# One level of Strassen's scheme for the output product of a hybrid attention layer

## The reference, cut to what matters

```python
merged = jax.nn.sigmoid(mg_a + b_gate[0]) * y_a + jax.nn.sigmoid(mg_b + b_gate[1]) * y_b
sub = jnp.einsum('bsd,de->bse', merged, w_out)              # 512 x 2048 by 2048 x 2048
out = layer_norm(DN_ALPHA * x.astype(jnp.float32) + sub.astype(jnp.float32), ln_g, ln_b)
```

## Time and profile before

| | |
|---|---|
| median of 3 runs | 1430.04 us |
| the profiled execution, its own time | 1427.57 us |
| its span, first to last instruction | 1425.8 us |
| mean granted TensorE clock | 0.997 |
| PE busy, share of the span | 98% |
| POOL, ACT, DVE busy | 49%, 35%, 26% |
| DMA moved, mean rate | 141.02 MB, 99 GB/s |

### The profile page before, as it was taken

One profiled execution on the slowest core, in us unless ns is written; L12 is line 12 of the kernel. 1 busy time (PEld: TensorE's weight loads), 2 busy tenths in 40 slices (PEclk: granted clock), 3 DMA queues, 4 the chain that ended last, 5 costly groups with the idle time before them and its releaser, 6 DMA issues.

```text
span 1425.8 us, 20252 instructions
## 1 busy us (share of the span) xinstructions
PE 1400.8 (98%) x6692; PEld 1185.1 (83%) x6692; DVE 368.2 (26%) x733; ACT 505.7 (35%) x694; POOL 701.7 (49%) x534
## 2 busy tenths in 40 slices
PE   9999999999999999999999999999999999999996
PEld 7878888778988988898898888888888888888885
DVE  5866565642030112203101101010010100400116
ACT  5455455443342343334234322222222222412122
POOL 4533333355445645544453455355553545554446
PEclk9999999999999999999999999999999999999998
DMA  8422221242333323233342334243342433393222
GB/s 258 122 60 74 79 78 45 73 143 70 89 90 85 89 77 97 66 87 88 85 116 66 88 94 112 74 118 88 88 118 74 118 84 88 113 269 107 91 74 118
DMA packets 191674, 141.02 MB, mean 99 GB/s; under 512 B 17296, under 2 KB 179344, under 8 KB 190736
## 3 DMA queue, kind: packets, MB, share of 16 engines
q1 hardware_dynamic: 191632, 140.47, 34.2%
HBM read 136.21 MB, written 4.19 MB: 98 GB/s over the span
## 4 chain that ended last, share of the span: by engine, by line
PE 92%; DVE 3%; issue 2%; ACT 1%; POOL 0%; DMA 0%; POOLq 0%; DVEq 0%; SPq 0%; ACTq 0%
PE acc L1010 84%; PE ps_out L1090 2%; PE ps_out L1081 1%; PE ps_scores L1034 1%; PE ps_scores L1027 1%; PE ps_turn L1064 1%; PE ps_scores L1010 1%; PE ps_out L1010 1%; DVE q_split L865 1%; PE ps_turn L1069 0%; DMA raw<-xT 0%; ACT q_split L491 0%; POOL z L443 0%; PE ps_scores L1036 0%; PE ps_scores L1035 0%
## 5 line engine op out<-in xcount | busy, mean ns | idle before, releaser
L430 POOL TENSOR_TENSOR w_lo<-raw,w_hi 128x512 fp32r<-128x512 f32 x260 | 342.7, 1318 | 712.5 <-ACT w_hi L457 698.8
L1010 PE MATMUL acc<-x_hi,w_hi 128*128 128x512 f32 x1216 | 479.3, 394 | 2.6 <-DVE q_a L723 2.6
L1010 PE MATMUL acc<-x_hi,w_lo 128*128 128x512 f32 x1216 | 474.3, 390 | 0.0
L1010 PE MATMUL acc<-x_lo,w_hi 128*128 128x512 f32 x1216 | 473.9, 390 | 0.0
L457 ACT ACTIVATE w_hi<-raw 128x1024 fp32r<-128x1024 f32 x256 | 267.8, 1056 | 447.9 <-PE acc L1010 421.3
L431 POOL TENSOR_TENSOR w_lo<-raw,w_hi 128x512 fp32r<-128x512 f32 x260 | 353.0, 1358 | 0.0
L1010 PEld LDWEIGHTS acc<-x_hi,w_lo 128*128 128x128 f32 x1216 | 228.3, 188 | 48.4
L1010 PEld LDWEIGHTS acc<-x_hi,w_hi 128*128 128x128 f32 x1216 | 228.6, 188 | 46.6 <-DVE q_a L723 3.2
L1010 PEld LDWEIGHTS acc<-x_lo,w_hi 128*128 128x128 f32 x1216 | 228.6, 188 | 43.5
L1010 PE MATMUL acc<-w_hi,x_hi 128*128 128x384 f32 (+1 forms) x512 | 185.3, 362 | 0.0
L1010 PE MATMUL acc<-w_hi,x_lo 128*128 128x384 f32 (+1 forms) x512 | 185.2, 362 | 0.0
(11 more groups left out here) (160 smaller groups left out, 1066.1 us busy)
## 6 DMA issues: line engine op xcount, KB each, us to landing
raw<-w_in SPq DMA_DIRECT2D x384, 128.0 KB, 2.3
raw<-w_in SPq DMA_DIRECT2D x256, 96.0 KB, 2.5
raw<-w_out SPq DMA_DIRECT2D x128, 128.0 KB, 2.9
raw<-w_in SPq DMA_DIRECT2D x64, 192.0 KB, 2.7
raw<-w_pa SPq DMA_DIRECT2D x64, 128.0 KB, 2.3
raw<-xT SPq DMA_DIRECT2D x8, 512.0 KB, 4.7
raw<-w_in SPq DMA_DIRECT2D x64, 64.0 KB, 2.2
raw<-w_pb SPq DMA_DIRECT2D x64, 64.0 KB, 2.5
```

Source lines behind the costliest of these rows:

```text
L430: nc.gpsimd.tensor_tensor(dst[:, left], raw[:, slot, left], hi[:, left].bitcast(F32), ALU.subtract)
L1010: ins = nc.tensor.matmul(into[:, 0:cols], s, m, start=start and k == 0, stop=stop and k == n - 1)
```

## The change

The product is computed as `[[x11, x12], [x21, x22]]` by `[[b11, b12], [b21, b22]]` with blocks of 256 rows by 1024 features on the left and 1024 by 1024 on the right. Seven block products P1 to P7 take the place of eight. In code:

- **Sums of weights.** Four sums q1 to q4 of w_out's blocks (4 MB each) are made in DRAM by 16 DMAs of 2 MB issued by POOL: 8 plain copies and 8 that add to what is there (`accum_op`). One is issued after every 12 jobs of stages A, B and M, each after a wait for the one before. SP waits for all 16 before the first load of stage O.
- **Sums of merged.** DVE makes four sums of `merged` per pair of feature tiles (`left_sums`), ACT and DVE split them (`left_high`, `left_low`). Pairs 0 and 1 are done in the last iteration of M, pairs 2 and 3 in jobs 0 to 3 of stage O. The blocks that the last three products need are split in jobs 17 to 27 (`end_high`, `end_low`).
- **Stage O** becomes 56 jobs (before: 32) of the same 512 KB. A job serves two blocks of 128 rows, so it has 12 matmuls. Jobs 0 to 15 and 16 to 31 fill P1, P6, P7, P5 of one half of the columns, all eight PSUM banks; jobs 32 to 39 are P4, 40 to 55 are P2 and P3.
- **Low parts.** In stage O POOL makes w_lo of the even jobs and of jobs 1 and 3, DVE that of the odd jobs from 5 on (`low_dve`), one instruction of 1024 columns.
- **Adding up.** DVE combines the products into z: `left_products` (12 operations, 8 of them freeing banks) at job 15 and 31, `left_sides` (8 operations, 6 of them with two inputs in SBUF) one job later, `add_product` for P4, P2, P3.
- **Loads of x** are issued behind jobs 7 to 10, the LayerNorm rows behind job 39.
- **LayerNorm** of row blocks 2 and 3 is moved ahead, to jobs 42 to 45, all of its 2048 columns on DVE; blocks 0 and 1 keep the tail's form.

The diff, cut to its core:

```diff
-O_ITERS, O_JOBS = 4, 8
+O_UNITS, O_JOBS = 2, 56
+SUMS, SUMS_APART = 16, 3
+P1, P6, P7, P5, P4, P2, P3 = range(7)
+FIRST_JOB = (0, 16)
+QUARTER_JOB = (32, 36)
+LAST_JOB = (40, 48)
+BANKS = {P1: (0, 1), P6: (2, 3), P7: (4, 5), P5: (6, 7), P2: (0, 1), P3: (2, 3)}
+POOL_LOW = [q for q in range(O_JOBS) if q % 2 == 0 or q < 5]
+LN_ROWS = (2, 3, 0, 1)
+END_HIGH = (17, 19, 21, 23, 25, 27)
-LN_SPLIT = (1024, 896, 896, 1408)
+LN_SPLIT = (D, D, 896, 1408)
...
+def bank_o(product, unit, t):
+    return 4 + 2 * unit + t if product == P4 else BANKS[product][t]
...
+    for n in range(O_UNITS):
+        for q in range(16):
+            k, h = divmod(q, 2)
+            steps += [(FIRST_JOB[n] + q, (P1, P6, P7, P5)[c], n, t, ((k, SEQ * (c % 2)),), k == 0, k == HALF - 1)
+                      for c in (2 * h, 2 * h + 1) for t in range(2)]
...
+            def jobs_o():
+                sp.wait_ge(summed, 16 * SUMS)
                 for q in range(O_JOBS):
-                    job(job_o(n), False, q, load_o(n, q))
-                    if first and q == 4:
+                    low_ready(sp, q - RING)
+                    for dst, src in reversed(list(load_o(q)(raw[:, q % RING, :]))):
+                        sp.dma_start(dst, src).then_inc(raw_in[q % RING], 16)
+                    if q == 7:
                         sp.wait_ge(full[3], fills_m(3, M_ITERS))
-                    if first and q >= 4:
+                    if 7 <= q < 7 + NR:
+                        sp.dma_start(z[:, q - 7, :], x_v[q - 7]).then_inc(x_in[q - 7], 16)
+                    if q == 39:
+                        sp.wait_ge(full[7], fills_o(7) + 2)
+                        sp.dma_start(g_row[:], ln_g.partition_broadcast(P)).then_inc(row_in, 16)
+                        sp.dma_start(b_row[:], ln_b.partition_broadcast(P)).then_inc(row_in, 16)
...
+            sums = [(dst[:, part], src[:, part], add) for part in (slice(0, HALF // 2), slice(HALF // 2, HALF))
+                    for dst, src, add in ((q1, b11, False), (q3, b22, False), (q1, b12, True), (q3, b12, True),
+                                          (q2, q1, False), (q2, b22, True), (q4, q2, False), (q4, b21, True))]
+            apart = SUMS_APART
+            for n, (dst, src, add) in enumerate(sums):
+                with pool.Fori(n * apart, (n + 1) * apart) as i:
+                    for s in range(RING):
+                        low(w_lo[:, s, :], s, w_hi[:, s, :], i * RING + (PRO_JOBS + s))
+                if n:
+                    pool.wait_ge(summed, 16 * n)
+                if add:
+                    nc.gpsimd.dma_start(dst, src, accum_op=ALU.add).then_inc(summed, 16)
+                else:
+                    nc.gpsimd.dma_start(dst, src).then_inc(summed, 16)
...
+            def left_high(n):
...
+                act.wait_ge(merged_ready, HALF + 2 * n + 2)
+                nc.scalar.activation(s_hi[:, ks, 0, :], merged[:, ks, 0:2 * P], ACT.Copy).then_inc(s_hi_ready, 1)
+                act.wait_ge(s_diff, n + 1)
+                act.wait_ge(s_two, n + 1)
+                act.wait_ge(s_three, n + 1)
+                for c in (3, 1, 2):
+                    nc.scalar.activation(s_hi[:, ks, c, :], s_sum[:, ks, c, :], ACT.Copy).then_inc(s_hi_ready, 1)
...
+            def jobs_o():
+                for q in range(O_JOBS):
+                    if q + AHEAD < O_JOBS:
+                        high(JOB_O, q + AHEAD)
+                    if q in (0, 2):
+                        left_high(2 + q // 2)
+                    if q in END_HIGH:
+                        end_high(END_HIGH.index(q))
...
+            def left_products(n):
...
+                for t in range(2):
+                    p6, p6_free = filled(P6, n, t)
+                    if n:
+                        dve.wait_ge(z_scaled, 6 * n)
+                    nc.vector.tensor_copy(sum_two[:, t, :], held[t]).then_inc(free[bank_o(P1, n, t)], 1)
+                    dve.wait_ge(free[bank_o(P1, n, t)], fills_o(t) + n + 1)
+                    nc.vector.tensor_tensor(sum_two[:, t, :], p6, sum_two[:, t, :], ALU.add).then_inc(p6_free, 1)
...
+            def jobs_o():
+
+                for q in range(O_JOBS):
+                    if q + AHEAD < O_JOBS:
+                        low_dve(q + AHEAD)
+                    if q in (0, 2):
+                        left_sums(2 + q // 2)
+                    if q in (1, 3):
+                        left_low(2 + q // 2)
+                    if q in END_HIGH:
+                        end_low(END_HIGH.index(q))
+                    for n in range(O_UNITS):
+                        if q == FIRST_JOB[n] + 15:
+                            left_products(n)
+                        if q == FIRST_JOB[n] + 16:
+                            left_sides(n)
+                        if q == QUARTER_JOB[n] + 4:
+                            for t in range(2):
+                                add_product(P4, n, t)
+                    if q == 42:
+                        row_moments(0, 2, 8)
+                    if q == 43:
+                        row_scale(0)
+                        row_near(0, 2)
+                    if q == 44:
+                        row_moments(1, 3, 8)
+                        row_far(0, 2)
+                    if q == 45:
+                        row_scale(1)
+                        row_near(1, 3)
+                        row_far(1, 3)
+                    if q == LAST_JOB[0] + 7:
+                        for t in range(2):
+                            add_product(P2, 0, t)
+                            add_product(P3, 0, t)
```

More of the change, by code:

```diff
@@ L620, in iter_m @@
                     if last_iter and group == 2 and job == 8 and bank == 1:
-                        merged_high(0, 4, 12)
-                        merged_high(4, 8, 12)
+                        left_high(0)
                     if last_iter and group == 2 and job == 9 and bank == 1:
[L624 to L630, removed]
@@ L632, in iter_o @@
[L632 to L635 removed]
+                        left_high(1)
+            def left_high(n):
+                ks = slice(2 * n, 2 * n + 2)
+                if n == 0:
+                    act.wait_ge(full[3], fills_m(3, M_ITERS - 1) + 1)
+                act.wait_ge(merged_ready, HALF + 2 * n + 2)
[5 more added lines that the diff above has]
+                    nc.scalar.activation(s_hi[:, ks, c, :], s_sum[:, ks, c, :], ACT.Copy).then_inc(s_hi_ready, 1)
@@ new lines, in end_high @@
+            def end_high(n):
+                part, ks = divmod(n, 2)
+                ks = slice(4 * ks, 4 * ks + 4)
+                rows = slice(HALF + ks.start, HALF + ks.stop)
+                if part == 2:
+                    act.wait_ge(s_four, ks.stop // 2)
+                    act.wait_ge(s_lo_ready, ks.stop)
+                    dst, src = merged_r[:, ks, 0:2 * P], merged[:, ks, 2 * P:SEQ]
+                else:
+                    act.wait_ge(full[3], fills_m(3, M_ITERS))
+                    dst, src = end_hi[:, part, ks, :], merged[:, rows, 2 * P * part:2 * P * part + 2 * P]
+                    act.wait_ge(s_four, ks.stop // 2)
+                nc.scalar.activation(dst, src, ACT.Copy).then_inc(end_hi_ready, 1)
@@ new lines, in low_dve, with row_part, filled @@
+            def low_dve(q):
+                if q not in POOL_LOW:
+                    dve.wait_ge(hi_done, JOB_O + q + 1)
+                    s = q % RING
+                    nc.vector.tensor_tensor(w_lo[:, s, :], raw[:, s, :], w_hi[:, s, :].bitcast(F32), ALU.subtract)\
+                        .then_inc(lo_done_dve, 1)
+            def row_part(r, column, n):
+                c = column * QUAD + n * SEQ
+                return z[:, r, c:c + SEQ]
+            def filled(product, n, t):
+                bank = bank_o(product, n, t)
+                dve.wait_ge(full[bank], fills_o(bank) + fill_o(product, n) + 1)
+                return banks[bank], free[bank]
```

388 lines of the change are left out of this document (258 added, 130 removed).

## The result

| | before | after |
|---|---|---|
| median of 4 runs | 1429.71 us (1427.52 to 1431.1) | 1453.89 us (1452.05 to 1456.57) |
| profiled execution, time | 1427.6 us | 1454.56 us |
| its span, mean granted clock | 1425.8 us, 0.997 | 1452.6 us, 0.985 |

A forecast was written before the change was run, and what follows sets the result against it. Stage O was taken as bound by its number of matmuls, all else hidden. Terms -21.8 + 1.8 + 9.3 + 9.5 + 4.2 + 4.7 + 0.9 = +8.6 gave 1436.2 us, 1438.7 in medians; range 1419 to 1460.

The forecast's parts named there:

- The clock in the new gaps: Rival, chance 0.07: TensorE at 1.2 GHz for one job after each wait at jobs 10, 19, 40; 8.2 us more, 1447.
- Removed matmuls: Stage O: 672 matmuls, 96 fewer at 0.227 us each, -21.8 us.
- Sums of merged, job 3: Stage O, jobs 0 to 3: ScalarE's copies wait for VectorE's sums, delaying job 3; +1.8 us, bounds 0 and 4.
- T: The forecast's time zero at the start of stage O, when bank 3 is full; later steps are counted from it.
- Loads of x: Stage O, jobs 10 to 12: loads of x push the job loads behind them; +9.3 us, bounds 0 and 12.
- Adding up: Jobs 15 and 31: VectorE's combining delays low parts of jobs 19 and 35 and bank 4; +9.5 us, bounds 4 and 16.
- LayerNorm rows, job 40: Stage O: 2 MB of rows ahead of load 40 make job 40 late; +4.2 us, bounds 0 and 6.
- LayerNorm of blocks 2 and 3: Jobs 42 to 45: VectorE's normalising delays P2's banks, which TensorE waits for; +4.7 us, bounds 2 and 8.
- Tail: After the last matmul: the last block gets two banks between block 0 and its moments; +0.9 us, bounds 0 and 2.
- the DRAM sums' rival: Rival, chance 0.15: the DRAM sums stall the stages before stage O; 24 us more, 1463.
- DRAM sums: Stages before O: the DMAs summing weights cost TensorE nothing; 0 us, upper bound 24.
- Loads beside x: Rival, chance 0.25: at jobs 8 to 12 and 40 loads interleave with x and rows; 13.5 us less, 1425.2.

The follow-up runs named there:

- g_long: The kernel before, with TensorE waiting at the start of stage O's last three iterations for seven added VectorE copies of 512 columns: 1454.51 us.
- e4_x_apart: The changed kernel with the four loads of x behind jobs 5, 8, 11 and 14 instead of 7 to 10: 1448.98 us.
- e2_pool_low: The changed kernel with the low parts of jobs 19, 35 and 49 made by GpSimd instead of VectorE: 1442.08 us.
- e6_banks: The changed kernel with P4 in PSUM banks 0 to 3 instead of 4 to 7: 1452.61 us.
- e1_no_sums: The changed kernel without the 16 DRAM sums, loading plain blocks of w_out in their place: 1459.21 us.
- f_three: f_two with P4's first unit in banks 0 and 1, its second in 6 and 7, and the second sums and copies at jobs 6 and 8: 1427.25 us.
- f_two: The changed kernel with GpSimd low parts at jobs 19 and 35, casts first, x loads, left sums and LayerNorm spread, P4 in banks 0 to 3: 1428.44 us.

## Why the prediction was wrong

The sign was right, the time in the range, the size not: +24.2 us in medians where the sum had +8.7.

- **The clock in the new gaps, taken as nothing in the sum and given 0.07 as a rival: this is the step that failed.** It measured 13.3 us. The rival's own price, 3 x 2.72 = 8.2, had the size per gap right (2.8 to 2.9 us measured behind four of the five, 1.6 behind job 10) and three gaps instead of five. What misled was the earlier trace rows: one execution in which the gap of 3.2 us left the clock alone. All 13 profiled executions of this study together hold 90 gaps of 1.8 us or more, start to start, behind their first 30 us. All 30 of 3.6 and more were followed by 7 to 14 matmuls at the lower level, 1.6 to 3.0 us. The one of 3.55 in stage A was so in 10 of 13. Of the 47 shorter ones 12 were, with 6 to 8 matmuls, and 35 were not, the longest 3.33; 13 of the 35 are the gap of 2.1 at 305 in stage A. The shortest of the 12 is 1.95 long, but two more gaps of 0.7 stand between it and the slow matmuls; the shortest with no other gap between is 2.54. One row could not show that. The sum had waits of 7.3, 5.6, 4.2 and 4.7 in it, all longer than the gap that the row excused; g_long shows what they bring. The Trainium skill, TensorE: Matmul & The Clock Gate, Part 1, says that an idle engine drops to half the clock; the trace agrees for the long gaps, and I had quoted it beside the rival and not let it into the sum.
- **Removed matmuls**: -21.8, right (672, 0.227 each at the full clock).
- **Idle time in total**: the terms of the stage gave 29.5 (all but the tail), 31.4 measured. Close, but as a sum of errors that cancel, and with 1.9 us at jobs 0 and 2 that no term had:
- **Sums of merged, job 3**: 1.8 forecast, 4.5 waited. Mis-sized: job 3's low part was ready at T+14.7 instead of T+10.0. The sums were put at 0.7 each and two took 1.77 beside GpSimd: 2.0 of the 4.7 us. They began at T+4.3 instead of about T+2.3, since VectorE was in a low part of 2.85 us until T+1.0 and had two tiles of `merged` to make, not one: 2.0. GpSimd's two operations took 3.6 instead of 2.6 beside VectorE. The forecast's own steps, 0.7, 1.0 and three times 0.7, make T+3.8 and not 4.4, and with sums of 1.0 they give 2.7 more at most, not the bound of 4. The paragraph on the shared port named such slow operations for `left_sides` and left them out here.
- **Loads of x**: 9.3 forecast, 3.9 waited at job 10 and next to nothing at jobs 11 and 12. Oversized: PE came to job 10 at T+36.8 instead of T+29.0, mostly by what jobs 0 to 3 had lost, and the job was ready at T+40.8 instead of T+36.3. That the loads of x push the job loads behind them was right: the casts of jobs 8 to 11 start 6.4, 5.7 and 5.3 us apart, and in e4_x_apart job 10's gap is gone.
- **Adding up**: 5.6 forecast at job 19, 4.2 waited; 3.9 at jobs 32 and 35, 1.8 + 2.6 waited. Right in place and cause (e2_pool_low, e6_banks).
- **LayerNorm rows, job 40**: 4.2 forecast, 3.2 waited. **LayerNorm of blocks 2 and 3**: 4.7 forecast, 1.5 + 4.1 waited at jobs 47 and 48. **Tail**: 0.9, measured 1.0.
- **The range**: the forecast's own part, 1427 to 1450, is narrower than its bounds added up (1414 to 1456), and the measured time lies above it. It is inside the whole range only by the part that the DRAM sums' rival had added, and that rival did not occur.
- **DRAM sums**: 0, right (e1_no_sums, and the windows). That "before T nothing moved" held for the work; T itself came 2.5 us late for reasons that also strike kernels without the change.
- **Loads beside x** (rival, 0.25): did not occur; job 10 was waited for.

What stays open: why e1_no_sums is 5 us slower than after, and why of f_three's 4.8 us in stage O and tail only 2.3 stand in the medians. The first 30 us differ between executions of kernels that are the same there: PE waits 0.9 us for x_lo in before's, 1.7 in f_three's, 3.7 in f_two's. f_three's runs spread over 8.4 us, before's over 1.9, and no experiment here separates that.

## What to carry to other kernels

A TensorE that has never been idle has a clock term of zero that says nothing about the kernel after a change which makes it wait: price a new gap with its own length and, as here in all 30 cases of 3.6 us and more and in some of 2 to 3.6, 1.6 to 3.0 us at the lower level behind it, and read that from several executions, since one can be lucky. When an algorithm halves the matmuls per loaded byte, list for each job what every helper engine must do at the new pace; here the arithmetic saved (21.8 us) was spent twice over on chains that the old pace had hidden, and removing one gap often moved a part of the wait to a later job (job 3's to job 5, job 10's to 12 and 16, jobs 47 and 48's to 54 and 55). No single edit won back more than 11.8 us; spreading the extra work over many jobs and engines won 26.6: 1453.9, 1433.1, 1428.4, 1427.3.

## What the hardware did that I had not expected

- The clock behind one and the same gap differs between executions: the 3.55 us in stage A left a granted clock of 1.00 in three of 13 profiled executions and a lower one in ten (0.50 to 0.70 from 275 to 280 in nine; 0.83 in f_two, whose gap ends at 278.3). From this gap to the next it took 34.3 us in the three, 35.9 in seven and 37.2 to 37.3 in three: 1.6 or 3.0 us, of the size by which before's profiled execution lies below its median, 2.1.
- VectorE pays too when it works beside GpSimd: 0.68 to 1.77 us for 512 columns from two SBUF inputs, while GpSimd goes from 1.29 to 1.73.
- DMAs from DRAM to DRAM, 2 MB each, landed in 14.9 us at the median of the twelve that read w_out, four plain and eight adding, and in 10.0 at the median of the four plain copies within q_sum. From 750 to 1150, at a DMA share of 0.46 instead of 0.33, they delayed no matmul.
